# Twelve-layer two-block model on one core: where the second block's mixers turn queries, keys and the state-space output

## The reference

```
proj = rmsnorm(x) @ w_in          # split: gm_u, gm_v, ssm_z, ssm_xbc, ssm_dt, da_q, da_k, da_v, gates
y_a  = chunked_spatial_gating(gelu(gm_u), gelu(gm_v), ...)            # width 512
y_b  = rmsnorm(ssd_scan(...) * silu(ssm_z), norm_g)                   # width 1024
q, k = rope(rmsnorm(da_q)), rope(rmsnorm(da_k))                       # per head of 64
y_c  = rmsnorm(softmax(q1 k1) v - lam * softmax(q2 k2) v) * (1 - lam_init)   # width 512
g    = sigmoid(gates)                                                 # 3 x 1024
x    = x + (g0*(y_a @ w_a) + g1*(y_b @ w_b) + g2*(y_c @ w_c)) @ w_out
```

## Time and profile before

| what | value |
|---|---|
| runs of the kernel before | 2418.91 us median of 3 (2418.38 to 2423.98) |
| the profiled execution's own time | 2418.16 us |
| its span, first to last instruction | 2416.4 us |
| mean granted TensorE clock | 0.989 |
| PE busy | 2338.3 us, 97% of the span |
| DVE, ACT, POOL busy | 60%, 54%, 14% |

### The profile page before, as it was taken

How to read it: one execution, slowest core, us unless ns; L and a number is a source line. 1 busy time by engine, 2 the same in 40 slices (tenths; PEclk the granted TensorE clock), 3 DMA queues, 4 the chain that set the end, 5 groups by cost and what they waited for, 6 DMA issues and landing times.

```text
span 2416.4 us, 36753 instructions
## 1 busy us (share of the span) xinstructions
PE 2338.3 (97%) x15344; PEld 2089.0 (86%) x15344; DVE 1457.0 (60%) x2241; ACT 1311.5 (54%) x1966; POOL 332.5 (14%) x307
## 2 busy tenths in 40 slices
PE   7999999998999999999999999989999999899999
PEld 6799888787899878998789988889899898898998
DVE  6655555555644547446765477565687675555875
ACT  5554465554544556445554466464655675555654
POOL 0100032211100313001010003413000023430000
PEclk9999999999999999999999999999999999999999
DMA  6255543333455534555255553334455543344553
GB/s 259 97 200 192 189 160 140 132 130 105 175 192 190 193 122 166 187 186 200 91 189 191 192 172 143 135 109 178 172 191 192 185 164 134 128 142 173 192 190 125
DMA packets 58182, 398.94 MB, mean 165 GB/s; under 512 B 6816, under 2 KB 7072, under 8 KB 11680
## 3 DMA queue, kind: packets, MB, share of 16 engines
q1 hardware_dynamic: 56864, 393.75, 45.1%
q10 hardware_dynamic: 1152, 2.83, 0.3%
HBM read 395.51 MB, written 1.05 MB: 164 GB/s over the span
## 4 chain that ended last, share of the span: by engine, by line
PE 59%; DVE 7%; ACT 5%; POOL 2%; issue 2%; ACTq 0%; DVEq 0%; POOLq 0%
PE b L1252 10%; PE b L1254 10%; PE b L1253 10%; PE b L1156 7%; PE b L1157 7%; PE b L1158 7%; PE b L1161 4%; DVE wlo L1908 3%; PE b L1165 2%; ACT whi L1549 2%; DVE xb L2201 1%; ACT b L1545 1%; PE b L1223 1%; PE b L1224 1%; POOL xn L2603 1%
## 5 line engine op out<-in xcount | busy, mean ns | idle before, releaser
L1908 DVE TENSOR_TENSOR wlo<-raw,whi 128x2048 fp32r<-128x2048 f32 x362 | 840.9, 2328 | 482.7 <-ACT whi L1549 482.2
L1549 ACT ACTIVATE whi<-raw 128x2048 fp32r<-128x2048 f32 x362 | 690.3, 1911 | 426.0 <-PE b L1254 240.9
L1252 PE MATMUL b<-xh,whi 128*128 128x256 f32 x2560 | 726.4, 284 | 0.8 <-DVE wlo L1908 0.8
L1254 PE MATMUL b<-xh,wlo 128*128 128x256 f32 x2560 | 714.9, 279 | 0.0
L1253 PE MATMUL b<-xl,whi 128*128 128x256 f32 x2560 | 714.1, 279 | 0.0
L1252 PEld LDWEIGHTS b<-xh,whi 128*128 128x128 f32 x2560 | 483.5, 189 | 6.1 <-DVE wlo L1908 2.7
L1253 PEld LDWEIGHTS b<-xl,whi 128*128 128x128 f32 x2560 | 484.3, 189 | 1.9
L1254 PEld LDWEIGHTS b<-xh,wlo 128*128 128x128 f32 x2560 | 483.8, 189 | 0.0
L1156 PE MATMUL b<-whi,xh 128*128 128x512 f32 x640 | 262.4, 410 | 1.5 <-DVE wlo L1908 1.5
L1156 PE MATMUL b<-whi,oh 128*128 128x512 f32 x656 | 259.7, 396 | 0.6 <-DVE ol L2192 0.6
L1157 PE MATMUL b<-wlo,oh 128*128 128x512 f32 x656 | 256.5, 391 | 0.0
(11 more groups left out here) (234 smaller groups left out, 2954.4 us busy)
## 6 DMA issues: line engine op xcount, KB each, us to landing
raw<-in_w SPq DMA_DIRECT2D x362, 1024.0 KB, 4.8
gt<-in_rows SPq DMA_DIRECT2D x8, 512.0 KB, 4.0
bt<-in_rows SPq DMA_DIRECT2D x8, 512.0 KB, 4.9
abq<-in_rows ACTq DMA_DIRECT2D x2, 768.0 KB, 6.0
x<-in_x SPq DMA_DIRECT2D x1, 1024.0 KB, 6.3
bc<-in_rows SPq DMA_DIRECT2D x4, 256.0 KB, 6.0
out<-x SPq DMA_DIRECT2D x4, 256.0 KB, 2.2
msk<-in_masks SPq DMA_DIRECT2D x1, 768.0 KB, 21.3
```

What stands on the lines that cost most here:

```text
L1252: pe.matmul(out, wh[:, k, cs], ah[:, kk, :], start=kk == 0 and s == 0, stop=False, skip_group_check=True)
L1254: last = pe.matmul(out, wl[:, k, cs], ah[:, kk, :], start=False, stop=final and k == 3, skip_group_check=True)
L1549: return ac.activation(out, i, ACT.Copy)
L1908: ve.tensor_tensor(B.wlo[r][:, :], B.raw[r][:, :], B.whi[s][:, :], ALU.subtract).then_inc(sem["loV"], 1)
```

## The change

The query's turn moves from the flush behind k's projection to the point in `turned("k")` right after k's rope is put in the list. Key's turn comes 13 yields after that in place of 8, and two more yields pass before the attention may start. `ssm_out` writes the four `yparts` itself, six yields after the last `norm_y` and three yields apart, so they stand ahead of the attention in the `side` list. Each piece is now made without `full`: ACT scales from the bank straight to the high half, and DVE computes bank x gain - high half in four instructions of 128 x 128. The pieces of y's first half (q = 0) go to a new buffer `yq`, which takes the place of `xs` in SBUF; those of the second half go to `oh` and `ol`, blocks 4 to 7, which `branch(0, d)` does not read. `head_norm` gets a parameter `gap`; the norm of the attention's output uses 6 (roots six yields after the squares, scaling three yields later) in place of 2.

```diff
-    def head_norm(self, key, buf):
+    def head_norm(self, key, buf, gap=2):
         self.counts("squares", key)
         self.step("head_squares", key, buf)
-        yield
-        yield
+        for _ in range(gap):
+            yield
...
         self.step("head_roots", key, buf)
-        yield
+        for _ in range(gap // 2):
+            yield
...
                 self.rope((part, u), part, "two")
-                for _ in range(8):
+                if part == "q":
+                    return
+                self.turn(("q", u), "q", ("q", u))
+                done.append("q")
+                for _ in range(13):
                     yield
                 self.turn((part, u), part, (part, u))
+                for _ in range(2):
+                    yield
                 done.append(part)
...
                 self.step("norm_y", l, t)
+            for _ in range(6):
+                yield
+            for t in range(2):
+                for q in range(2):
+                    self.aux(("yturn", l, t, q))
+                    self.counts("yhi", (l, t, q))
+                    self.step("yparts", l, t, q)
+                    for _ in range(3):
+                        yield
             seen["y"] = True
...
-            yield from self.head_norm(("sub", u), "yo")
+            yield from self.head_norm(("sub", u), "yo", 6)
...
-        for t in range(2):
-            for q in range(2):
-                self.aux(("yturn", l, t, q))
-                self.counts("yhi", (l, t, q))
-                self.counts("ylo", (l, t, q))
-                self.step("yparts", l, t, q)
...
-        ah, al = B.act(src[1]) if src[0] == "x" else (B.oh, B.ol)
+        if src[0] == "x":
+            ah, al = B.act(src[1])
+        elif src[2] == 1 and half == 0:
+            ah, al = B.yq[:, 0, :, :], B.yq[:, 1, :, :]
+        else:
+            ah, al = B.oh, B.ol
...
@@ def yparts(l, t, q) in scalar_program @@
-        last.then_inc(sem[f"empty{b}"], 1)
-        a.wait_ge(f"empty{b}", n + 1)
-        copy(B.oh[:, 4 * q:4 * q + 4, 128 * t:128 * t + 128],
-             f.rearrange("p (k n) -> p k n", k=4)).then_inc(sem["yhi"], 1)
+        last.then_inc(sem["yhi"], 1)
...
@@ def yparts(l, t, q) in vector_program @@
-        ve.tensor_tensor(B.ol[:, 4 * q:4 * q + 4, sl], B.full[:, q, :].rearrange("p (k n) -> p k n", k=4),
-                         B.oh[:, 4 * q:4 * q + 4, sl], ALU.subtract).then_inc(sem["ylo"], 1)
+        for k in range(4):
+            kk = 4 * q + k
+            last = ve.scalar_tensor_tensor(out=to[:, k, sl], in0=B.bank[b][:, 128 * k:128 * k + 128],
+                                           scalar=g[:, kk:kk + 1], in1=h[:, k, sl], op0=ALU.mult, op1=ALU.subtract)
+        last.then_inc(sem[f"empty{b}"], 1)
...
-        self.xs, self.y = sb("xs", [128, 2, D]), sb("y", [128, 2, D])
+        with ExitStack() as steps:
+            self.xs = sb("xs", [128, 2, D], F32, steps)
+        self.yq = sb("yq", [128, 2, 4, 256], F32R)
+        self.y = sb("y", [128, 2, D])
```

More of the change, by code:

```diff
@@ L1204, in source_ready @@
             for t in range(2):
-                p.wait_ge("ylo", mark["ylo", (l, t, half)])
+                b, n = use["yturn", l, t, half]
+                p.wait_ge(f"empty{b}", n + 1)
         else:
@@ L1860, in yparts @@
         g = B.colp(f"sng{l}")
-        f = B.full[:, q, :]
+        to = B.oh[:, 4:8, :] if q else B.yq[:, 0, :, :]
         a.wait_ge(f"full{b}", n + 1)
[L1863 to L1867, removed]
         for k in range(4):
             kk = 4 * q + k
-            last = act(f[:, 128 * k:128 * k + 128], B.bank[b][:, 128 * k:128 * k + 128], ACT.Identity,
+            last = act(to[:, k, 128 * t:128 * t + 128], B.bank[b][:, 128 * k:128 * k + 128], ACT.Identity,
                        scale=g[:, kk:kk + 1])
-        last.then_inc(sem[f"empty{b}"], 1)
-        a.wait_ge(f"empty{b}", n + 1)
-        copy(B.oh[:, 4 * q:4 * q + 4, 128 * t:128 * t + 128],
-             f.rearrange("p (k n) -> p k n", k=4)).then_inc(sem["yhi"], 1)
+        last.then_inc(sem["yhi"], 1)
     def mparts(l, j):
@@ L2410, in yparts @@
     def yparts(l, t, q):
-        sl = slice(128 * t, 128 * t + 128)
+        b, n = use["yturn", l, t, q]
+        g, sl = B.colp(f"sng{l}"), slice(128 * t, 128 * t + 128)
+        h, to = (B.oh[:, 4:8, :], B.ol[:, 4:8, :]) if q else (B.yq[:, 0, :, :], B.yq[:, 1, :, :])
         v.wait_ge("yhi", mark["yhi", (l, t, q)])
-        ve.tensor_tensor(B.ol[:, 4 * q:4 * q + 4, sl], B.full[:, q, :].rearrange("p (k n) -> p k n", k=4),
-                         B.oh[:, 4 * q:4 * q + 4, sl], ALU.subtract).then_inc(sem["ylo"], 1)
+        for k in range(4):
[3 more added lines that the diff above has]
+        last.then_inc(sem[f"empty{b}"], 1)
     def branch(l, b_, d):
@@ L2583, in head_squares @@
             g.wait_ge(f"empty{b}", n + 1)
-            for q in range(2):
-                g.wait_ge("ylo", mark["ylo", (l, 1, q)])
+            g.wait_ge("stat_v", mark["stat_v", ("sums", "k", key[1])])
         else:
@@ L2809 @@
         "hhi", "hlo", "cva", "cvv", "gate", "xb", "vnorm", "wdh", "wdl", "lamv", "wst", "dtv", "dav", "xsg", "ea",
-        "xde", "offg", "built", "decays", "yam", "yahi", "yalo", "squares", "headn", "gz", "yn", "yog", "yhi", "ylo",
+        "xde", "offg", "built", "decays", "yam", "yahi", "yalo", "squares", "headn", "gz", "yn", "yog", "yhi",
         "mgg", "mgv", "mhi", "mlo"]
```

## The result

| what | before | after |
|---|---|---|
| median of the runs on the same chips | 2421.44 us (2418.38 to 2424.09, 4 runs) | 2391.02 us (2390.21 to 2391.68, 4 runs) |
| ratio | 1 | 0.987 [0.9857, 0.9883] |
| profiled execution, its span | 2418.16, 2416.4 us | 2391.34, 2389.5 us |
| mean granted TensorE clock | 0.989 | 0.994 |
| mixer stretch, first layer | 136.57 us | 119.90 us |

The mixer stretch runs from the first matmul of the last step of k's projection to the first column step of `branch(2,0)`; it holds all three places that the prediction speaks of. The change made the kernel 1.3% faster, 30.4 us by the medians.

What follows compares the result with a forecast made beforehand. PE bounds the kernel, busy 97% of the span, losing idle and half-clock time: 32.8 us lost less 0.7 gives 32.1; 2418.16 less that is 2386.1, plus 0.75 gives 2386.8 us; own range 2382 to 2390, full range 2381 to 2396.

Steps and rivals of the forecast that it cites:

- three places: PE's losses in each mixer, first layer: q's turn 6.29 us, k's turn 4.41, pieces of y 6.13.
- 0.7 for the split pieces: Cost in both layers of extra returns from transposes to column steps, 0.09 us each, at y's pieces and k's turn.
- my discount of 0.9 us: Second layer's pieces of y taken 0.9 us cheaper, since its L1161 waits are 2.95 us in place of 3.85.
- q's turn: Moved behind step 5 at 1561.1; q's rope ends at 1558.49, margin 2.6 us.
- First piece of y: Behind step 3 of `branch(0,0)` at 1570.4; `norm_y` ends at 1570.15, thinnest margin, 0.25 us.
- k's turn against the rope: Behind step 6 of `gate(0,1)` at 1582.2; k's rope ends at 1578.98, margin 3.2 us.
- Its bank: k's turn needs bank 6, which holds piece 3 until DVE is done at 1581.4; margin 0.8 us.
- First score: Behind step 8 at 1585.9; needs banks 4 and 5, so piece 4 at 1584.9; margin 1.0 us.
- Rival 1: k's turn or first score still waits, as DVE's long subtractions stretch POOL's rope: 1 to 4 us per layer, chance 0.16.
- Rival 2: PE waits at first piece for `norm_y`: late 1 to 4 us, chance 0.05; over 14 us, a loss, chance 0.04.
- Rival 3: PE's saving is taken back by late weights or POOL's chain: within 0.3% of before, 2412 to 2426, chance 0.03.
- The attention's output: Its norm moves about eight steps later; scaling must end before `opart`, 14 us behind; claimed cost none.

Runs made afterwards that it cites:

- q_only: Kernel before with only q's turn moved; k's turn and y's pieces as before: 2420.4 us beside 2420.99, ratio 0.9995.
- y_early: Changed kernel without the six yields ahead of the pieces of y: 2405.13 us, ratio 0.9928.
- qk_only: Kernel before with both turns placed as in the change, pieces of y in old place and form: 2409.42 us, ratio 0.9951.
- y_late: Changed kernel with the new form of the pieces and `yq`, but all four in a row behind `branch(0,1)` as before: 2408.64 us, ratio 0.9943.
- y_only: Changed kernel with q's and k's turns back in their old places: 2406.02 us, ratio 0.9942.
- gap_two: Changed kernel with the old gap of 2 in the norm of the attention's output: 2390.67 us, ratio 0.9864.
- before_b: Kernel before, unchanged, profiled again: 2423.44 us.
- before_c: Kernel before, unchanged, profiled once more: 2425.81 us.
- shift_one: Changed kernel with 16 extra transposes in the first layer's feed-forward part, shifting everything behind by 1.8 us: 2392.48 us.
- shift_two: Changed kernel with 32 extra transposes in the first layer's feed-forward part, shifting everything behind by 3.5 us: 2395.46 us.
- k_early: Changed kernel with 8 yields ahead of k's turn in place of 13: 2408.18 us, ratio 0.9933.

## Why the prediction was right

**What bounds.** Right. Only PE's idle time and its half-clock time gave anything; both are gone from the mixer stretches. In the first profile of before PE's waits in the first layer's stretch sum to 9.5 us and the clock is at 0.50 for 13.7 us, of which half, 6.8, is lost: 16.4 us, beside the 16.67 gained.

**The three losses.** 32.8 us less 0.7 for the split pieces was the sum, 32.98 was measured. The first layer came to 16.67 where 16.83 - 0.36 = 16.47 was forecast. The second came to 16.31 where 15.93 - 0.36 = 15.57 was: both layers end at the same 119.90 and stood at 136.57 and 136.21 before, so my discount of 0.9 us for its shorter wait for a bank should have been 0.36. What I had not seen is how far the losses depend on each other: q_only keeps 2.7 of 12.6 us. (A slip in the words at k's turn: the column step at 1588.65 is the third behind the score and not the fourth; the sum rightly counts two.) The method (length of the stretch less its undisturbed content) gives the price of all three together, and not a share for each.

**The margins.** The walk was right within 0.2 us at each step of PE, over 32 us. q's turn: 2.6 us to spare, as forecast. First piece of y: 0.25 forecast, 0.38 measured; y_early shows what lies behind it. k's turn against the rope: 3.2 and 3.06. Its bank: 0.8 and 1.3. First score: 1.0 and 1.9. DVE's pieces 1.11 us each (1.15), ACT's 1.14. DVE was a few tenths to 0.8 us earlier than I had it.

**Rival 1** (the rope, stretched by DVE's subtractions, ends too late) did not come in the changed kernel. Its two instructions of 2.37 us lie beside the two low halves of weights of 2.40 and 2.45. Beside the first piece, at 1579.88 to 1580.99, the rope's instructions took their 0.46 (the rows at 1580.22 and 1580.76). The third low half starts at 1586.55, when the rope is over. But its mechanism is real, and it came where the pieces of y did not stand between the low halves: in qk_only and y_late the rope met four low halves and k's turn waited 1.9 to 2.0 us in each layer, and y_only shows such a wait of 1.62 us. The argument against it, that the rope meets the same two subtractions as before, holds only for the whole change. These waits lie within the 1 to 4 us a layer of this rival. By the rule of the Trainium skill that the prediction names ("SBUF — State Buffer", "SBUF: two separate sides"), pieces that read one operand from a bank block nobody; the trace agrees, with 0.46 us.

**Rival 2** (the first piece too early) did not come, with 0.38 us to spare. y_early put it there: 6.7 and 7.9 us a layer, of which 5.2 is idle time. The prediction's price for lateness, "beyond about 2 us the half clock adds some 2 more", has no such edge in the runs: behind 1.50 us the clock fell in one execution and not in another, behind 1.96 it did not and behind 1.92 it did within one.

**Rival 3** (little change) is q_only's case: q's turn by itself measures as no change. The argument for it, PE gains 6.3 us and POOL only 2.92, is what happens when k's turn keeps its place. The change moves it too.

**The attention's output.** Its squares on POOL took 6.07 us, not the 4 that I allowed as twice the squares of k. There were still 9 us between `subscale` (1657.24) and `opart` (1666.26), and gap_two shows the price as nothing.

**Where it was off.** The forecast was 4.2 us under the median. The first part of it is the last step, "the median of the runs shown is 0.75 us above the profiled one": the three runs shown (2418.38, 2418.91, 2423.98) belong to the two groups of time that the first block makes, and I took the lower for the base. Of the 4.2 us, 2.5 are this base: before's median in the measurement is 2421.44, half of its four runs from the upper group, and not 2418.9. The other 1.7 are the gain, 30.4 us between the medians in place of 32.1, since all four runs of the changed kernel are of its upper group. The sum taken from before_b's 2423.44 gives 2391.3, and the changed kernel's profiled execution took 2391.34; from before_c's 2425.81 it would give 2393.7. The forecast's own range, 2382 to 2390, had no term for it and misses the median by 1 us, though the 5.6 us between the runs shown could be read; the full range, 2381 to 2396, holds it.

**What stays open.** Why an execution falls into one group or the other. The start of the trace goes with it: in before's first profile, in q_only and in shift_one the clock rises at 10 us and is down again from 13 to 24; in after, before_b and before_c it rises once, at 18.4 to 18.9. shift_two lies between, down again only from 14 to 18, and has two of the three falls that tell the groups apart. It does not go with it strictly: qk_only starts like shift_two and has only the fall at 110 us, and of the four profiles where the clock rises once at 23 to 24 us, gap_two, y_early and k_early have all four extra falls and y_late two. So the times form two groups, but the profiles hold any number from none to four of these falls. What decides it, no run here shows.

## What to carry to other kernels

Where PE works an in-order list, price a wait as the length of the disturbed stretch less the undisturbed price of what it holds; at q's turn 6.3 us were lost behind gaps of 3.15 us in all. Then place the step by walking both clocks, PE's and the feeder's, to the next place as well, and look what the feeder itself runs beside there: a turn moved alone gave 2.7 of 12.6 us, and the whole list placed right gave 33 in the two stretches. Before the base of a forecast is fixed, look whether the runs shown fall into groups, and hold profiles of the same group against each other.

## What the runs showed of the hardware

The same idle spot of PE, 1.50 us at 454 us, left the granted clock at 1.00 (2.4 GHz) in one execution and took it to 0.50 (1.2 GHz) in another of the same kernel, and the 2.41 us near 940 did the same. The last step of k's projection started at 1552.73, 1558.45 and 1559.17 in three executions of one kernel; the second has four falls more ahead of it (111, 455, 875, 940 us) and a shorter slow start. A gap of 1.5 to 2.4 us thus had no fixed price here: an execution paid for it or did not, and two gaps of 1.96 and 1.92 us in one execution (y_late) differed too. How long the half clock lasts varied as well: 3.4 or 6.8 us behind the same wait of 5.2 us (y_early). The times of this kernel of 2400 us form two groups some 5 us apart. And a scaling of a bank by four instructions on DVE beside POOL's rope did not slow POOL (0.46 us for 128x128), where low halves of weights did: 2.37 us in place of 0.32 for 128x64, 2.39 in place of 0.46 for 128x128, and in the changed kernel each of the two ended 0.2 us behind its low half.
